# Large SBUF tiles at multiples of 256 bytes from the first tile instead of at multiples of 64

## The reference

```python
hn = _rmsnorm(h, g_mix)                       # h = x, [1, 1024, 1024]
proj = hn @ w_in                              # q, k, v of two head groups, gates, forget logits
o_nsa = _nsa_mixer(...)                       # 8 heads: compressed + selected + window branches, gated
o_fox = _fox_mixer(...)                       # 8 heads: causal softmax with a forget bias
mixed = concat([_rmsnorm(o_nsa, beta_nsa), _rmsnorm(o_fox, beta_fox)])
h = h + mixed @ w_out
u = _rmsnorm(h, g_ffn)
for e in range(16):                           # combine: 1 group of 4, then 2 of its 4 experts per token
    hid = silu(u @ w_gate_e[e]) * (u @ w_up_e[e])
    y = y + combine[..., e:e + 1] * (hid @ w_down_e[e])
h = h + y
gate = sigmoid(_rmsnorm(h, g_ple) @ w_ple_gate + b_ple_gate)
h = h + gate * (p @ w_ple_proj)
return _rmsnorm(h, g_final)
```

## Time and profile before

| what | us |
|---|---|
| timed executions | 1449.14, 1461.89, 1464.17 |
| their median | 1461.89 |
| profiled execution, its time | 1452.9 |
| its span | 1451.2 |
| TensorE busy in it | 1351.5 |
| VectorE busy | 773.9 |
| ScalarE busy | 619.8 |

### The profile page before, as it was taken

The page is one execution under the profiler, slowest core; times in us unless marked ns, Lnnn a source line. Parts: engine busy times, 40 slices in busy tenths (PEclk is TensorE's granted clock), DMA queues, the critical chain, the costliest instruction groups (busy, mean ns, idle before and its releaser), DMA issues. The chain is left out here.

```text
span 1451.2 us, 23331 instructions
## 1 busy us (share of the span) xinstructions
PE 1351.5 (93%) x7609; PEld 1133.5 (78%) x7610; DVE 773.9 (53%) x1575; ACT 619.8 (43%) x938; POOL 192.2 (13%) x219
## 2 busy tenths in 40 slices
PE   5899999989999999999889986999999999948996
PEld 4688888988888888888778864788888888837775
DVE  5734112646555554445353336678655767846762
ACT  5312111224333334444542213578644767845542
POOL 2100000115222123343000000000000000001100
PEclk9999999989999999999999977999999999969999
DMA  7233332122100111553232219699976979784411
GB/s 262 75 111 84 102 92 87 43 72 50 24 23 23 38 45 46 133 124 69 66 112 88 94 51 356 238 345 411 358 260 246 351 314 348 312 313 143 164 69 44
DMA packets 110994, 224.37 MB, mean 155 GB/s; under 512 B 17469, under 2 KB 44461, under 8 KB 110910
## 3 DMA queue, kind: packets, MB, share of 16 engines
q1 hardware_dynamic: 96694, 180.90, 36.7%
q0 software_dynamic: 10272, 30.57, 5.9%
q10 hardware_dynamic: 3944, 11.81, 2.2%
HBM read 178.66 MB, written 36.24 MB: 148 GB/s over the span
## 5 line engine op out<-in xcount | busy, mean ns | idle before, releaser
L1426 ACT ACTIVATE att_prob<-att_ps_s 128x512 f32<-128x512 f32 (+1 forms) x240 | 134.5, 561 | 240.0 <-PE att_ps_s L1356 200.0
L1471 DVE CUSTOM_DVE_ANT_0 att_ps_m<-att_ps_m,tok_maskb 128x128 f32<-128x128 f32 (+3 forms) x260 | 111.0, 474 | 140.7 <-PE att_ps_m L1303 137.7
L2097 DVE TENSOR_TENSOR exp_g_lo<-exp_g_raw,exp_g_hi 128x1024 fp32r<-128x1024 f32 x128 | 146.8, 1220 | 12.8 <-ACT exp_g_hi L2006 12.8
L1374 PE MATMUL att_ps_o<-tok_vsw,att_prob 128*128 128x65 f32 x1056 | 142.4, 277 | 0.8 <-DVEq L1515 0.5
L140 PE MATMUL moe_ps_g<-exp_g_hi,moe_xT_hi 128*128 128x512 f32 x336 | 136.2, 405 | 3.9 <-DVE exp_g_lo L2097 2.5
L1374 PEld LDWEIGHTS att_ps_o<-tok_vsw,att_prob 128*128 128x128 f32 x1056 | 134.5, 196 | 3.8 <-ACT att_prob L1426 1.0
L141 PE MATMUL moe_ps_g<-exp_g_lo,moe_xT_hi 128*128 128x512 f32 x336 | 134.4, 400 | 0.0
L142 PE MATMUL moe_ps_g<-exp_g_hi,moe_xT_lo 128*128 128x512 f32 x336 | 134.0, 399 | 0.0
L2006 ACT ACTIVATE exp_g_hi<-exp_g_raw 128x1024 fp32r<-128x1024 f32 x128 | 123.6, 1046 | 22.2 <-issue 11.5
L140 PE MATMUL prj_ps_w<-prj_hT_hi,att_w_hi 128*128 128x512 f32 x256 | 103.9, 406 | 5.4 <-ACT att_w_hi L492 2.1
L141 PE MATMUL prj_ps_w<-prj_hT_lo,att_w_hi 128*128 128x512 f32 x256 | 102.8, 402 | 0.0
(11 more groups left out here) (468 smaller groups left out, 2908.1 us busy)
## 6 DMA issues: line engine op xcount, KB each, us to landing
exp_g_raw<-in_w_gate_e SPq DMA_DIRECT2D x128, 256.0 KB, 5.1
exp_g_raw<-in_w_up_e SPq DMA_DIRECT2D x128, 256.0 KB, 5.9
exp_d_raw<-in_w_down_e SPq DMA_DIRECT2D x64, 512.0 KB, 7.7
y_rows<-moe_y ACTq DMA_DIRECT2D x21, 512.0 KB, 6.1
att_w_raw<-in_w_in SPq DMA_DIRECT2D x16, 512.0 KB, 3.7
att_w_raw<-feat SPq DMA_DIRECT2D x30, 256.0 KB, 5.1
feat<-att_w_out POOLq DMA_DIRECT2D x14, 512.0 KB, 2.9
y_rows<-moe_zeros SPq DMA_DIRECT2D x10, 512.0 KB, 10.9
```

What stands on the lines that cost most here:

```text
L1374: last = nc.tensor.matmul(ps_o[:, u % 2, (q % 4) * HV:(q % 4 + 1) * HV], prob[:, b % PT, at + (q - qa) * P:at + (q - qa + 1) * P], value(k ...
L1426: nc.scalar.activation(prob[:, b % PT, 0:w], ps_s[:, b % ST, 0:w], ACT.Exp, scale=-1.0).then_inc(expd, 1)
L1471: last = nc.vector.tensor_tensor_reduce(p[:, at:at + w], p[:, at:at + w], K["maskb"][:, mask_at:mask_at + w], 1.0, -2.0 * NEG, ALU.add, AL ...
L2097: nc.vector.tensor_tensor(g_lo[:, ch % GR], g_raw[:, ch], g_hi[:, ch % GR].bitcast(F32), ALU.subtract).then_inc(s_glo, 1)
```

## The change

`Scope` now keeps count of the bytes handed out since the first tile (`Scope.taken`, which a scope that ends sets back). A tile of 1 KB or more gets a filler ahead of it up to the next multiple of 256 of that count; a smaller tile gets none, and the filler behind tiles is gone, so that small tiles start at multiples of 32. `build` sets the count to 0 first.

```diff
+    taken, ROW = 0, 256
...
-        self.nc, self.name, self.ctx, self.sems = nc, name, ExitStack(), []
+        self.nc, self.name, self.ctx, self.sems, self.base = nc, name, ExitStack(), [], Scope.taken
...
+        Scope.taken = self.base
         return self.ctx.__exit__(*a)
...
     def sb(self, name, shape, dt=F32):
-
-        tile = self.ctx.enter_context(self.nc.sbuf_tensor(f"{self.name}_{name}", shape, dt))
-        used = math.prod(shape[1:]) * (2 if dt is BF16 else 4)
-        if 0 < used % 64 <= 32:
-            self.ctx.enter_context(self.nc.sbuf_tensor(f"{self.name}_{name}_fill", [P, 8], F32))
-        return tile
+        size = -(-math.prod(shape[1:]) * (2 if dt is BF16 else 4) // 32) * 32
+        fill = -Scope.taken % self.ROW if size >= 1024 else 0
+        if fill:
+            self.ctx.enter_context(self.nc.sbuf_tensor(f"{self.name}_{name}_fill", [P, fill // 4], F32))
+        Scope.taken += fill + size
+        return self.ctx.enter_context(self.nc.sbuf_tensor(f"{self.name}_{name}", shape, dt))
...
     K = {}
+    Scope.taken = 0
     with Scope(nc, "all") as outer:
```

## The result

The changed kernel takes 1438.67 us (median of 20 executions, 1436.0 to 1451.66), the kernel before, run beside it, 1457.59 us (20 executions, 1449.14 to 1465.58). The ratio is 0.9886 with a 95% interval of 0.9861 to 0.9912: 18.9 us at the medians' difference, 1.1% faster. The forecast of 1459.0 and its range of 1443 to 1474 are wrong, and rival 1 (*operands in phase*, 1440 us, -19.2 us) is what happened. The two profiled executions took 1452.9 and 1437.5 us, with spans of 1451.2 and 1435.8.

The account below looks back on a forecast made before the run. The prediction took TensorE's matmul pace as the bound and summed four terms of 0 (TensorE; VectorE and ScalarE; small tiles; DMA) to 1452.9 us, then chose 1459 us between the executions' mean and median; range 1443 to 1474.

Parts of the forecast that it names:

- rival 1: Matmuls whose two operands lie equally far from a multiple of 256 run at the last stage's pace: -19.2 us; chance 0.08.
- What bounds the kernel: Whole kernel: TensorE, busy 93% of the span, sets the end by the pace of its matmuls.
- TensorE's operands: Matmuls in all stages: operand addresses cost nothing, term 0, with bounds of +2.8 and -19.2 us.
- the 284 and 283 pair: Projection's second part: same stationary activations at 128, value weights at 128 or 0, 284 and 283 ns, so no effect.
- The second pair: Products with the values: 65-column slices starting 260 bytes apart all average 273 ns, so a moving operand's start costs nothing.
- The bound from below: Expert, projection and mix stages: 2664 matmuls each gain 7.2 ns, together -19.2 us.
- Rival 3: Last stage loses its pace because its operands leave 0: +2.8 us, 1462; chance within the forecast's 0.84.
- Rival 4: All tiles: they stay 128 from a multiple of 256, so the change does nothing it names; chance within the forecast's 0.84.
- VectorE, ScalarE and small tiles: Splits, evictions and tiles below 1 KB: both terms 0, bounds -1 to +1 us and 0 to +1 us.
- DMA: Loads and stores: tile starts at 0, 64 or 128 cost the same within 2%, term 0.
- the cover: Expert weight loads: issued 15.5 us before their split, leaving about 9 us to absorb slower landings.
- Rival 2: Weight loads: 2 KB rows take 1/8 longer and use up the lead, deciding from 11%; 1479 us, chance 0.06.

Follow-up runs that it names:

- e4: Changed kernel with the activations of the projection, mix, expert and last stages 128 bytes further, weights unmoved; ratio 1.0018 to the kernel before.
- e2: Changed kernel with 128 bytes ahead of the first tile, so all large tiles lie on true multiples of 256; ratio 0.9917 to the kernel before.
- e5: Changed kernel with real 32-byte fillers that put small tiles back at multiples of 64, large tiles unmoved; ratio 0.9925 to the kernel before.
- e1: Kernel before with 192 bytes ahead of the expert stage's tiles, moving only its activations from 64 to 0, where the weights are; ratio 0.9965.
- w1: Kernel before with 384 of 512 columns in the six middle chunks of gate and up, leaving out part of the work; span 1423.3 us.
- w2: As w1, but with 192 bytes ahead so the expert activations start at 0 like the weights; span 1421.1 us.
- e3: Changed kernel with tile counts rounded to 64 instead of 32 bytes; a wrong edit that also shifted large tiles; ratio 1.0015 to the kernel before.
- c1 to c3: Changed kernel with each stage's activations shifted by other multiples of 32 bytes against the weights, three kernels; spans 1462.1, 1457.9 and 1449.5 us.
- c4: Changed kernel with only the lo parts of the stationary activations 128 bytes further in mix, expert and last stages; span 1458.2 us.

## Why the prediction was wrong, point by point

**What bounds the kernel: right.** TensorE's pace set the end, and most of a change in pace went through to it: 15.7 us of shorter steps, 13.9 us of shorter span at the same clock (e4 against the changed kernel: 16.7 and 13.3). The waits of the earlier trace rows hardly moved. The same in the changed kernel (us in total, times, longest):

```profile
PE fin_ps_x L2641 <- PEq L169: 14.6, 1, 14.6
...
PE moe_ps_g L140 <- DVE exp_g_lo L2100: 2.5, 1, 2.5
```

**TensorE's operands: the step that failed.** The prediction took 0, "the value of the 284 and 283 pair, which holds all but the address equal". The pair does hold the address alone, and it told the truth about its own kind: 256 columns show no effect at any distance. But it was carried over to 512 columns, which are the ones that fill the kernel, and there the term is -15.7 us by the steps and -13.9 by the spans at the same clock, where the prediction had 0. (The medians give -18.9, with some 5 us of scatter in it.) The second pair, 65 columns, had the same fault and more of it. The bound from below had the right matmuls and a step that was too large: 2664 x 7.2 ns = 19.2 us, where means over whole groups give 5.2 to 6.2 ns, since the 0.2335 and 0.2263 of the earlier trace rows are two short stretches and the last stage's mean is 227.8.
The rows did hold the warning, and the prediction wrote it down: 7.2 ns between two stages "and I can't say why from the rows". An unexplained difference in the very width and engine that bound the kernel deserved more than the 0.08 that its one written-out explanation got. The objection against it rested on a width of which nothing in the time depended.

**Rival 3 and "all tiles 128 past a multiple": right facts, wrong weight.** The tiles are where the prediction put them, and e2 shows that 0 and 128 are the same to TensorE. The last stage keeps 227.8 ns. Rival 4 (the change does nothing it names, so nothing happens) had the right observation and the wrong conclusion: the distance to true multiples isn't what acts, the distance between partners is.

**VectorE, ScalarE and small tiles: right.** 684 ns after 683 and busy sums within 0.5 us; e5 and the second run of the change can't be told apart (0.9925, 0.9930).

**DMA: right for the time, wrong for the work.** The term 0 rested on shares of 6.4% that did not separate 0 from 64, and on 4.5 against 4.6 us. With nearly all of the loads' targets at 128 the traffic does cost more. Work of the load queue, its share times the span:

| | weights at 0 | weights at 128 |
|---|---|---|
| matmuls apart | before 36.7% x 1451.2 = 533 us | e4 37.2% x 1449.1 = 539 us |
| matmuls in phase | e2 36.9% x 1437.0 = 530 us; e1 37.0% x 1439.8 = 533 us | after 37.6% x 1435.8 = 540 us; second run 37.4% x 1441.5 = 539 us |

The rows of the table differ by 3 us at most, the columns by 6 to 10: it is the place, not the pace. That is some 1.4%. The other runs agree: w1 and w2, weights at 0, have 532 and 533 us; e3, e5 and c1 to c4, weights at 32 or 128, have 538 to 542. The packets of 2 KB alone took 89.5 ns in the mean before and 90.9 after, 1.6% more. The Trainium skill's page "DMA: Bandwidth & Descriptors", section "How a descriptor splits into AXI transactions", has a transfer that starts between two multiples of 256 pay for the bytes below its start; for the rows of 2 KB that was some 6% by its beats. The direction agrees; the 1.6% of the 2 KB packets is a quarter of it. Issues of the changed kernel (count, KB each, median us from issue to landing):

```profile
exp_g_raw<-in_w_gate_e SPq DMA_DIRECT2D x128, 256.0 KB, 6.5
exp_g_raw<-in_w_up_e SPq DMA_DIRECT2D x128, 256.0 KB, 7.4
exp_d_raw<-in_w_down_e SPq DMA_DIRECT2D x64, 512.0 KB, 9.7
```

The same three of the kernel before:

```profile
exp_g_raw<-in_w_gate_e SPq DMA_DIRECT2D x128, 256.0 KB, 5.1
exp_g_raw<-in_w_up_e SPq DMA_DIRECT2D x128, 256.0 KB, 5.9
exp_d_raw<-in_w_down_e SPq DMA_DIRECT2D x64, 512.0 KB, 7.7
```

The expert loads land 1.4 to 2.0 us later in a full queue (the second run of the change has 7.8 for down, so this median scatters more than the share does). Here the prediction's longest landing, 4.6 us, was read outside of the saturated stretch; the 7.7 us for down was on the same page. It did no harm, for the cover held. The load of a chunk and its split in the changed kernel, load queue and ScalarE:

```profile
955.49 0.34 SPq L1923 DMA_DIRECT2D exp_g_raw<-in_w_gate_e  x1
```

```profile
970.60 2.02 ACT L2009 ACTIVATE exp_g_hi<-exp_g_raw 128x1024 fp32r<-128x1024 f32 x2 [0.74 <-issue]
```

15.1 us from issue to split, after 15.5. The cover is thinner elsewhere, though. ScalarE's waits for the loads in the expert stage of the changed kernel (us in total, times, longest):

```profile
ACT exp_d_hi L2015 <- DMA exp_d_raw<-in_w_down_e: 9.9, 6, 5.1
...
ACT exp_g_hi L2009 <- DMA exp_g_raw<-in_w_up_e: 2.7, 3, 2.0
```

And of the kernel before:

```profile
ACT exp_g_hi L2006 <- DMA exp_g_raw<-in_w_up_e: 10.7, 4, 8.3
...
ACT exp_d_hi L2012 <- DMA exp_d_raw<-in_w_down_e: 0.3, 1, 0.3
```

The wait for gate and up comes and goes between runs (10.0 us in the second run of the change). The one for down is a trend, by one trace each: 0.3 us before, 6.4 and 6.6 with a faster TensorE alone (e1, e2), 6.5 to 7.9 with the weights at 128 alone (e4, c1 to c3), 9.7 to 10.1 with both (the changed kernel twice, e5). That the faster TensorE frees the buffers sooner and so asks for the same bytes in less time fits this, but wasn't tested by itself. TensorE's own waits show nothing of it: the split still runs far enough ahead. Rival 2 named a real mechanism with a price that was too high, and its point of decision, 11%, was never near.

**Range and chances.** The range's lower end, 1443, was meant to reach towards rival 1 and stopped 4 us short of the median that came. By luck of the scatter that median lay further out than the mechanism puts it: 1457.59 - 13.9 = 1443.7, just inside. That doesn't save the forecast, whose mechanism was no change at all, and it is the same luck that puts rival 1's 1440 so near to 1438.67: its -19.2 us is a third too large beside 13.9. With all the cases on one side bound by one open difference in the rows, -19.2 should have been inside it.

## What to carry to other kernels

Give tiles that meet in one wide float32 matmul (stationary and moving) starts that are equal modulo 256; it costs some bytes of filler, and 5 to 7 ns of 233 at 512 columns come back, in long unbroken runs of such matmuls. Where the kernel is bound by TensorE, most of it reaches the end; e1 shows that 192 bytes in front of one stage are enough for that stage. And when a row is used as evidence that something costs nothing, take it from the shape that fills the time, and measure the distance between starts, not the duration of one.

## What the runs showed of the hardware

- The pace of TensorE on float32 matmuls of 384 and 512 columns depends on the relative start of its two operands in a partition: 227 ns against 232 to 234 at 512 columns, 173.8 against 176.4 at 384 (these two from the seventh step of a run on), nothing at 256 and 288. A distance of 192 gave 229.1 in its one group. The Trainium skill's page "SBUF — State Buffer", section "SBUF: two separate sides", says that TensorE never waits on anyone at its SBUF ports; no run here shows it waiting on another engine there, but its pace depends on where its own two operands start.
- A stationary tile out of phase slows the step before its matmul and its own (232.5 and 233.5 ns) and spares the third (227.7). Why both is open.
- The gain needs a run of matmuls to set in: in w2 the first 384 column steps come 170 to 190 ns apart and only later ones steadily at 173 to 174. In gate and up of the changed kernel the first five steps of a run average 230.3 ns and the later ones 226.5; apart, in the kernel before, there is no such start (232.4 and 233.0). Why is open.
- The scatter between executions of this kernel follows TensorE's mean granted clock: at 0.965 to 0.967 the spans of the kernel before lie within 7 us, over all 52 executions (0.956 to 0.971) within 20.
- Loads into tiles 128 past a multiple of 256 cost the queue about 1.4% more work than into tiles on one: 538 to 542 us in the changed kernel (twice), e4, e5 and c1 to c4, 530 to 533 in the kernel before, e1, e2, w1 and w2. e3, 32 past one, has 542.
